# Output projection by token tile, with its norm per tile, ahead of the second FFN

## The reference

```
def modulate(h, s): return h * (1.0 + scl[:, s]) + shift[:, s]
h = swiglu(modulate(x, 0), w_ffn1_in, w_ffn1_out)
x = layer_norm(ALPHA * x + 0.5 * gate[:, 0] * h, ln_gain[0], ln_bias[0])
u = modulate(x, 1)
... # u @ w_in, pooling mixer and three attention branches
mix = concatenate([pool_out, nsa_out], axis=-1) @ w_out
x = layer_norm(ALPHA * x + gate[:, 1] * mix, ln_gain[1], ln_bias[1])
h = swiglu(modulate(x, 2), w_ffn2_in, w_ffn2_out)
x = layer_norm(ALPHA * x + 0.5 * gate[:, 2] * h, ln_gain[2], ln_bias[2])
```

## Time and profile before

| | |
|---|---|
| median of 3 runs | 1358.32 us (1356.65 to 1359.41) |
| the profiled execution, its time | 1361.54 us |
| its span in the profile | 1359.9 us |
| PE busy | 1287.4 us, 95% |
| DVE busy | 569.4 us, 42% |
| ACT busy | 445.3 us, 33% |
| POOL busy | 186.8 us, 14% |
| output projection starts | 848.3 us |
| third chunk of ffn2_in starts | 931.7 us |
| second half of FFN 2 starts | 1198.5 us |

### The profile page before, as it was taken

How to read it: one execution, slowest core, us unless ns; L and a number is a source line. 1 busy time by engine, 2 the same in 40 slices (tenths; PEclk the granted TensorE clock), 3 DMA queues, 4 the chain that set the end, 5 groups by cost and what they waited for, 6 DMA issues and landing times.

```text
span 1359.9 us, 25442 instructions
## 1 busy us (share of the span) xinstructions
PE 1287.4 (95%) x9688; PEld 1159.0 (85%) x9688; DVE 569.4 (42%) x966; ACT 445.3 (33%) x702; POOL 186.8 (14%) x369
## 2 busy tenths in 40 slices
PE   4999999999999997998879998989999999999997
PEld 3899999999999997997546666979999999988875
DVE  2422223222332366214558776584323323332466
ACT  2222222222211124224536655144222222233353
POOL 3000000000000022652372052033000000030000
PEclk8899999999999998999999999989999999999999
DMA  9544544545444343783651045222222232263463
GB/s 295 164 143 128 174 130 146 163 123 159 146 132 146 103 103 78 173 174 99 200 124 34 1 141 141 78 63 63 78 86 83 77 91 79 77 209 124 148 198 127
DMA packets 238769, 170.03 MB, mean 125 GB/s; under 512 B 46979, under 2 KB 227471, under 8 KB 238632
## 3 DMA queue, kind: packets, MB, share of 16 engines
q1 hardware_dynamic: 232159, 151.36, 38.8%
q0 software_dynamic: 6544, 17.82, 4.5%
HBM read 164.75 MB, written 8.63 MB: 128 GB/s over the span
## 4 chain that ended last, share of the span: by engine, by line
PE 86%; DVE 6%; ACT 4%; issue 1%; DVEq 1%; DMA 1%; SPq 0%; POOL 0%; POOLq 0%; ACTq 0%
PE ps L296 60%; PE ps L881 10%; PE ps L1116 3%; PE ps L2309 2%; PE ps L1125 1%; PE ps L1502 1%; PE ps L273 1%; ACT AR L1723 1%; DVE AR L2342 1%; PE ps L1610 1%; PE ps L1519 1%; DVE XT L461 1%; DVE UL L342 1%; DMA AR<-in_x_sample_dram 1%; PE ps L1573 1%
## 5 line engine op out<-in xcount | busy, mean ns | idle before, releaser
L296 PE MATMUL ps<-UH,WH 128*128 128x288 f32 x1680 | 361.0, 296 | 2.3 <-DVE WL L256 1.5
L296 PE MATMUL ps<-UH,WL 128*128 128x288 f32 x1680 | 357.9, 294 | 0.0
L296 PE MATMUL ps<-UL,WH 128*128 128x288 f32 x1680 | 357.5, 294 | 0.0
L256 DVE TENSOR_TENSOR WL<-RAW,WH 128x1024 fp32r<-128x1024 f32 x136 | 167.7, 1234 | 347.0 <-ACT WH L252 344.1
L296 PEld LDWEIGHTS ps<-UH,WH 128*128 128x128 f32 x1680 | 268.5, 188 | 2.8 <-DVE WL L256 1.8
L296 PEld LDWEIGHTS ps<-UL,WH 128*128 128x128 f32 x1680 | 269.5, 187 | 0.0
L296 PEld LDWEIGHTS ps<-UH,WL 128*128 128x128 f32 x1680 | 268.6, 188 | 0.0
L252 ACT ACTIVATE WH<-RAW 128x1024 fp32r<-128x1024 f32 x136 | 142.9, 1051 | 117.4 <-PE ps L296 109.0
L881 PE MATMUL ps<-WH,H 128*128 128x512 f32 x380 | 97.3, 398 | 0.0
L647 DVE TENSOR_TENSOR T<-MU,ps 128x576 f32<-128x576 f32 x44 | 33.2, 754 | 149.7 <-PE ps L296 149.0
L487 POOL TENSOR_TENSOR AR<-AR 128x576 f32<-128x576 f32 x12 | 19.8, 1649 | 544.9 <-ACT AR L406 482.3
(11 more groups left out here) (353 smaller groups left out, 1512.2 us busy)
## 6 DMA issues: line engine op xcount, KB each, us to landing
RAW<-in_w_ffn_in_dram SPq DMA_DIRECT2D x88, 512.0 KB, 4.9
AW<-in_w_ada_dram SPq DMA_DIRECT2D x56, 512.0 KB, 4.1
RAW<-in_w_ffn_out_dram SPq DMA_DIRECT2D x36, 512.0 KB, 3.4
AR<-in_w_ada_dram SPq DMA_DIRECT2D x7, 1024.0 KB, 10.9
RAW<-in_w_ffn_out_dram SPq DMA_DIRECT2D x16, 448.0 KB, 3.8
RAW<-in_w_in_dram SPq DMA_DIRECT2D x28, 256.0 KB, 4.1
AW<-in_w_ffn_out_dram SPq DMA_DIRECT2D x14, 512.0 KB, 3.5
AR<-in_cache_k_cmp_dram POOLq DMA_DIRECT2D x64, 64.0 KB, 2.6
```

What stands on the lines that cost most here:

```text
L256: nc.vector.tensor_tensor(WL[:, slot, :], RAW[:, slot, :], WH[:, slot, :].bitcast(F32), ALU.subtract).then_inc(split_done, 1)
L296: mm = nc.tensor.matmul(ps[:, 2 * uslot + h, 0:HT], W[:, wslot, k * P:(k + 1) * P], R[:, k0 + k, h * HT:(h + 1) * HT], start=(first and k ...
```

## The change

The output projection is done as the second half of FFN 2 is: activations stationary, weight rows moving. For each of 8 rows of weights, units 0 and 1 and the sample unit (US) get their matmuls; then unit 2 runs over all 8, then unit 3. The weights' parts lie in the place of H2 (`mix_w`), so nothing waits for a slot of WH and WL. The `turn_x` pieces move from the second half of FFN 2 to here, 3 behind each of rows 4, 5 and 6. The norm goes by unit, with the functions of the final norm: units 0, 1, then the samples, 2, 3. A new `xhat` writes the normed rows, PE turns them back to features (`early_turn`, `sample_turn`, `tile_turn`), ACT modulates them and writes UH (`rows_mod`, two instructions per feature tile, 256 columns for units 0 and 1 together, then 128 for unit 2, then 128 for unit 3), DVE writes UL (`rows_lo`). The first two chunks of ffn2_in run over 384 prompt tokens and the 64 samples, and then over the last 128 tokens (`first_rows`). The stage ln1 is gone. Gain and bias of ln1, which XT got on POOL, are applied to XA by POOL in the second half of FFN 2. The gate rows are made behind `first_pair` of w_in, for both gates (16 transposes, 4 ACT copies, 4 POOL DMAs), and 17 POOL DMAs read them back as tables before the norm. In `attn_pe`, `nat_pe` uses banks 4 to 7 and stands ahead of the wait for the pages' read-out, and two of the small transposes stand ahead of the wait for its own read-out.

```diff
-          ("w_in", 15, 8, 7), ("w_out", 8, 4, 4), ("ln1", 0, 1, 0), ("ffn2_in", 2 * FT, FT, FT),
+          ("w_in", 15, 8, 7), ("w_out", 8, 0, 0), ("ffn2_in", 2 * FT, FT, FT),
...
-        OBANK = {0: (4, 5), 1: (6, 7), 4: (4, 4), 2: (2, 3), 3: (0, 1)}
-        XA = AR2[:, 0:KT * T]
...
+                for m in range(KT):
...
+        def gate_rows_pool(pool):
+            for q, (src, _bank) in enumerate(GSRC):
+                pool.wait_ge(gt_rows, q + 1)
+                pool.dma_start(GROWS[q // 2, :, 512 * (q % 2):512 * (q % 2) + 512], src).then_inc(gt_out, 16)
...
+        def tokens_pool(pool):
+            pool.wait_ge(chunk_mm, CH0["ffn2_out"] + 2)
+            pool.wait_ge(mix_in, 16 * GATE_LOADS)
+            gain_tables(pool, 1, BX, mix_in)
+            gain_tables(pool, 2, BC, bc_in)
+            gate_tables(pool, 2, BC["gate"], BC["gate_s"], bc_in)
+            pool.wait_ge(mix_in, 16 * (GATE_LOADS + GAIN_LOADS))
+            for t in UNITS:
+                x = unit(XA, t)
+                nc.gpsimd.tensor_tensor(x, x, BX["gain" if t < 4 else "gain_s"], ALU.mult)
+                pool.drain()
+                nc.gpsimd.tensor_tensor(x, x, BX["bias" if t < 4 else "bias_s"], ALU.add).then_inc(xu_ready, 1)
...
+        def xhat(act, st, u, count):
...
+            act.wait_ge(nmr_ready, count)
+            nc.scalar.activation(unit(XA, t), unit(st.z, t), ACT.Identity, bias=NMR[:, t:t + 1],
+                                 scale=RST[:, t:t + 1]).then_inc(xh_ready, 1)
...
+        def mix_pe(pe):
...
+                src = US[:, k, :] if t == 4 else (UH, UL, UH)[q][:, k, t * P:(t + 1) * P]
+                for h in range(2):
+                    mm = nc.tensor.matmul(ps[:, OBANK[t][h] if t < 4 else 6 + h, :], src, mix_w(k, q // 2)[:, h * 512:(h + 1) * 512],
+                                          start=(k == 0 and q == 0), stop=(k == KT - 1 and q == 2))
+                return mm
...
+            for k in range(KT):
+                pe.wait_ge(hi_done, n0 + k + 1)
+                pe.wait_ge(u_split, 2 * KT + k + 1)
+                for t in (0, 1):
+                    part(k, t, 0)
+                    part(k, t, 1)
+                    if t == 0:
+                        pe.wait_ge(split_done, n0 + k + 3)
+                    mm = part(k, t, 2)
+                    if k == KT - 1:
+                        mm.then_inc(row_mm, 1)
+                        if t == 0:
+                            sample(k - 1).then_inc(chunk_mm, 1)
+                            sample(k).then_inc(row_mm, 1)
+                    elif t == 1:
+                        mm.then_inc(chunk_mm, 1)
+                if 0 < k < KT - 1:
+                    sample(k - 1)
+                if k == 4:
+                    pe.wait_ge(ln_out, KT)
+                if 4 <= k < KT - 1:
+                    for f in range(3 * (k - 4), 3 * (k - 3)):
+                        turn_x(pe, f)
+            for t in LATE:
+                if t == 2:
+                    pe.wait_ge(xa_ready, 9)
+                else:
+                    pe.wait_ge(hs_read, 1)
+                for k in range(KT):
+                    for q in range(3):
+                        mm = part(k, t, q)
+                    if k == KT - 1:
+                        mm.then_inc(row_mm, 1)
+                    j = (0 if t == 2 else KT) + k
+                    if j == 2:
+                        pair_product(pe, MIX)
+                    elif j == 6:
+                        pair_sums(pe, MIX, 0, SUMT[:, 4:5], row_sum)
+                    elif j == 8:
+                        pair_sums(pe, MIX, 1, SQT[:, 4:5], row_sq)
+                    elif j in (7, 9, 10, 11):
+                        early_turn(pe, (7, 9, 10, 11).index(j))
+                    elif j == 12:
+                        sample_turn(pe)
+                    elif j == 13:
+                        tile_turn(pe, 2, um_t, 4)
...
+        def early_turn(pe, f):
...
+                for t in range(2):
+                    mm = nc.tensor.transpose(ps[:, 2 + f % 2, (k % 2) * 256 + t * P:(k % 2) * 256 + (t + 1) * P],
+                                             XA[:, t * D + k * P:t * D + (k + 1) * P], IDN[:, :])
+            mm.then_inc(ue_t, 1)
...
+        def tile_turn(pe, t, done, count):
+            pe.wait_ge(xh_ready, count)
...
+            mm.then_inc(done, 1)
...
+        def rows_mod(act, i, j):
...
+                act.wait_ge(u_rows, j - 3)
+            nc.scalar.activation(ubuf(j), src, ACT.Identity, bias=ADA[:, SHIFT[i] + k, 0:1],
+                                 scale=ADA[:, SCALE[i] + k, 0:1]).then_inc(u32_act, 1)
+            act.drain()
+            nc.scalar.activation(UH[:, k, c0:c1], ubuf(j), ACT.Copy).then_inc(uh_rows, 1)
+        def rows_lo(dve, j):
+            k, (c0, c1) = j % KT, USPAN[j]
+            dve.wait_ge(uh_rows, j + 1)
+            nc.vector.tensor_tensor(UL[:, k, c0:c1], ubuf(j), UH[:, k, c0:c1].bitcast(F32), ALU.subtract).then_inc(u_rows, 1)
...
+        def mix_act(act):
+            for k in range(1, KT):
+                mix_hi(act, k)
+            for f, (t, h) in enumerate(XUNIT):
+                act.wait_ge(xa_t, f + 1)
+                nc.scalar.activation(unit(Z1, t)[:, h * 512:h * 512 + 512], ps[:, 4 + f % 2, :], ACT.Copy).then_inc(xa_ready, 1)
+            hi(act, *split_args("ffn2_in", 0))
+            act.wait_ge(row_mm, 5 * MIX.n + 2)
+            nc.scalar.activation(HSUM, ps[:, 6:8, :], ACT.Copy).then_inc(hs_read, 1)
+            squares_at(act, MIX, 0)
+            squares_at(act, MIX, 2)
+            xhat(act, MIX, 0, 1)
+            xhat(act, MIX, 2, 2)
+            squares_at(act, MIX, 1)
+            for j in range(4):
+                rows_mod(act, 2, j)
+            act.wait_ge(row_pair, 2 * MIX.n + 2)
+            deviation_at(act, MIX, 1, ps[:, 1, 1:2])
+            xhat(act, MIX, 1, 3)
+            rows_mod(act, 2, 4)
+            squares_at(act, MIX, 3)
+            for j in range(5, KT):
+                rows_mod(act, 2, j)
+            sample_rows_hi(act)
+            xhat(act, MIX, 3, 4)
+            hi(act, *split_args("ffn2_in", 1))
+            for j in range(KT, 2 * KT):
+                rows_mod(act, 2, j)
+            squares_at(act, MIX, 4)
+            xhat(act, MIX, 4, 5)
+            for j in range(2 * KT, 3 * KT):
+                rows_mod(act, 2, j)
+        def mix_dve(dve):
+            for k in range(1, KT):
+                mix_lo(dve, k)
+            pair_made(MIX)
+            dve.wait_ge(mix_in, 16 * GATE_LOADS)
+            dve.wait_ge(xa_ready, 9)
+            gated(dve, MIX, 0)
+            summed(dve, MIX, 0)
+            gated(dve, MIX, 2)
+            summed(dve, MIX, 2)
+            shift_at(dve, MIX, 0, 1)
+            dve.wait_ge(hs_mm, 1)
+            gated(dve, MIX, 1)
+            shift_at(dve, MIX, 2, 2)
+            summed(dve, MIX, 1)
+            lo(dve, *split_args("ffn2_in", 0)[:2])
+            dve.wait_ge(row_pair, 2 * MIX.n + 1)
+            mean_at(MIX, 1, ps[:, 1, 0:1])
+            for j in range(2):
+                rows_lo(dve, j)
+            gated(dve, MIX, 3)
+            for j in range(2, 4):
+                rows_lo(dve, j)
+            summed(dve, MIX, 3)
+            shift_at(dve, MIX, 1, 3)
+            for j in range(4, 7):
+                rows_lo(dve, j)
+            shift_at(dve, MIX, 3, 4)
+            sample_mod(dve, 2)
+            rows_lo(dve, 7)
+            sample_rows_lo(dve)
+            lo(dve, *split_args("ffn2_in", 1)[:2])
+            for j in range(KT, 2 * KT - 2):
+                rows_lo(dve, j)
+            for h in range(2):
+                gated(dve, MIX, 4, h)
+            summed(dve, MIX, 4)
+            for j in range(2 * KT - 2, 2 * KT):
+                rows_lo(dve, j)
+            shift_at(dve, MIX, 4, 5)
+            for j in range(2 * KT, 3 * KT):
+                rows_lo(dve, j)
...
+        def first_rows(pe):
...
+            for s in range(2):
+                w = (CH0[a] + s) % 2
+                pe.wait_ge(split_done, CH0[a] + s + 3)
+                for k in range(KT):
+                    if s == 0:
+                        pe.wait_ge(u_rows, KT + k + 1)
+                    for q, (W, R) in enumerate(((WH, UH), (WH, UL), (WL, UH))):
+                        nc.tensor.matmul(ps[:, 2 * s, 0:LATE_COL], W[:, w, k * P:(k + 1) * P], R[:, k, 0:LATE_COL],
+                                         start=(k == 0 and q == 0), stop=(k == KT - 1 and q == 2))
+                    if s == 1 and k == 1:
+                        tile_turn(pe, 3, ul_t, 5)
+                if s == 0:
+                    pe.wait_ge(us_rows, 1)
+                for k in range(KT):
+                    for q, (W, R) in enumerate(((WH, UH), (WH, UL), (WL, UH))):
+                        nc.tensor.matmul(ps[:, 2 * s + 1, P:P + TS], W[:, w, k * P:(k + 1) * P], R[:, k, TP:T],
+                                         start=(k == 0 and q == 0), stop=(k == KT - 1 and q == 2))
+            for s in range(2):
```

(91 more changed lines are left out.)

515 lines of the change are left out of this document (257 added, 258 removed).

## The result

The changed kernel takes 1376.2 us (median of 4 runs, 1371.9 to 1381.6), the kernel before 1358.9 beside it: ratio 1.0127, 95% interval 1.0102 to 1.0151. It is slower, as forecast, but by 17 us and not by 6, and outside the range of 1355.0 to 1369.5.

The account below looks back on a forecast made before the run. PE was taken as the bound (86% of the chain). Stretch +12.5 us (81.7 work, 13.0 waits, 1.2 clock), second half -5.0 and +0.4, pages -2.0, w_in +0.2: +6.1, so 1364.4 us against the median; range 1355.0 to 1369.5.

Parts of the forecast that it names:

- PE's work: From the projection's start to the third chunk of ffn2_in: matmuls and transposes of PE sum to 81.7 us.
- The main doubt: In first_rows: 64-column matmuls cost as much as 128-column ones, 0.11 us each, 10.6 us for 96.
- The clock: In the rebuilt stretch: 1.2 us added for a lowered clock, tied to the 6.9 us wait at unit 2's turn.
- more is lost: Rival: PE at half clock through most of first_rows and loads slower beside POOL's; +4, 1368.4 us, chance 0.12.
- The third turn of x: In the projection: PE waits 1.2 us for the weight-row splits; 2.2 with later turns, 4 if loads take 4.5.
- Unit 2's turn: At tile_turn of unit 2 in the norm: PE waits 6.9 us for ACT's xhat.
- DVE behind unit 3: Before unit 2's last rows: DVE gates and sums unit 3 ahead of the last two rows_lo; wait 2.7 us.
- Silu: Before the third chunk of ffn2_in: ACT's two Silu pieces make PE wait 0.7 us.
- The sum of the waits: All PE waits from the projection's start to the third chunk of ffn2_in: 13.0 us.
- second half: Second half of FFN 2: nine turns go, -5.0 us; unit 1 waits for DVE's last-chunk product, +0.4.
- behind the pages: From the pages' wait to the convolution: four of ten transpose groups and the small ones leave the path, -2.0 us.
- The gap in w_in: Behind the first pair of w_in: 16 gate-row transposes instead of 8 cost +0.2 us.

Follow-up runs that it names:

- e11: e8 with ACT making unit 2's xhat ahead of the samples' high part; 1355.3 us, ratio 0.9968 to the kernel before.
- e5: Kernel before plus three runs of 144 extra unused matmuls, of 64, 128 and 192 columns; 1417.5 us (one run).
- e2: Changed kernel with ACT reading out the first three turns of x before splitting the eighth weight row; 1367.3 us, ratio 1.0069.
- e12: Changed kernel with each projection weight row fetched by one DMA of 128 consecutive rows (output wrong, same work); 1370.2 us, ratio 1.0074.
- e8: e7 with early turns, samples' turn and first pair sum moved up in PE's list, ACT and DVE order following; 1355.7 us, ratio 0.9976.
- e4: Changed kernel with the samples' 64 columns joined to the late 128 in matmuls of 192; 1368.2 us, ratio 1.0065.
- e1: Changed kernel run again unaltered; 1378.1 us, ratio 1.0135 to the kernel before.
- e3: Changed kernel with POOL's 17 table DMAs held until the last weight row is split; 1373.0 us, ratio 1.0084.
- e7: Changed kernel with the edits of e2 and e4 together; 1360.2 us, ratio 1.0014 to the kernel before.
- e6: Kernel before with only the part behind the pages changed (nat_pe banks and place, two small transpose groups moved up); 1355.9 us, ratio 0.9979.
- e10: e8 with the one-DMA weight-row load of e9 added; 1378.2 us, ratio 1.0143 to the kernel before.
- e9: Changed kernel with each projection weight row fetched by one DMA into 128 partitions instead of two of 64; 1399.6 us, ratio 1.0295.

## Why the prediction was wrong in size

- **PE's work**: right. In e11, at full clock there, the projection, the turns and the products are within 0.7 us of their terms. The 384-column matmuls take 8.8 us in the changed kernel for 8.4. (Their 10.3 in e11 hold 1.4 of half clock behind the wait of 2.4, and 0.3 because some rows come from ACT and DVE one per 0.74 us.) The main doubt, 0.11 us for 64 and 128 columns, holds where the clock is full: 0.108 for 64 in the changed kernel, 0.112 for 128 in e5. The Trainium skill (TensorE: Matmul & The Clock Gate, Back-to-back issue gap) has about 81 ns per 128-column matmul in a stream of loads and matmuls; the runs of 64, 128 and 192 columns on 128 stationary ones here took 108 to 113 ns each. Its rule for the weight load (LDWEIGHTS), 107 ns, agrees with 0.108 to 0.112.
- **The clock: the step that failed.** "To these I add 1.2 for the clock." In the table above the changed kernel's rows exceed the work at full clock by about 8 us: 2.2 in the projection, 1.3 in the samples' turn, 0.8 in unit 2's, 4.0 in the last 48 matmuls. Sorted by place, 1.7 us stand behind the wait at the samples' turn and 2.6 behind the one at unit 2's turn (e2 and e12 remove the first together with its wait, e8 the second); the 4.0 stand behind the 64-column matmuls, where PE had been busy (e4, e5). The prediction had one fall of the clock, behind the wait at unit 2's turn, at less than half its price; there were three, and the dearest needs no wait. So the term of 1.2 should have been about 8, and this 7 is most of the 8.8 by which the stretch was missed. The rival "more is lost" had PE at half clock through most of `first_rows`, for +4 in all, and was given 0.12: the place was in part right (half clock over the last 48 matmuls, full clock over the 96 before), but it too was too small.
- **The third turn of x**: the mechanism was right, the load mis-sized. "3.4 us of load" came from the 2.7 of the earlier trace rows. Measured: 0.47 + 4.2. The wait was 6.0 (5.7 in e1) for 1.2, and all the waits for the turns of x 6.5 for 2.2. Three loads stand one behind the other on that chain, so 1.3 more for each is 3.9 more in all, which is nearly the difference; the prediction's own bound, 4 in all for loads of 4.5, was added up too low (three times 1.1 more makes 5.5). POOL is not the cause (e3), the two transfers of 64 partitions are (e12).
- **Unit 2's turn**: right, 6.4 for 6.9, with ACT's three waits at 1.6, 2.3 and 1.4 for 1.4, 2.2 and 1.5. ACT's rows of 256 columns took 0.95 to 0.97 us each for 1.05. e8 and e11 show that the wait is a matter of order: the same work without it.
- **DVE behind unit 3**: 0.5 for 2.7 in the profile, 1.8 in e1, 2.3 in e8 and 2.4 in e11. PE at half clock comes to it later, so that one loss covers another: in e1 the clock rises sooner behind unit 2's turn, PE reaches the first 384-column matmul 5.0 us after that turn's start for 6.3, and waits 1.3 longer for DVE's rows. For Silu there is no wait for the 0.7 forecast, and 0.6 once the clock is full (e4, e7, e8, e11).
- The sum of the waits, 13.7 for 13.0, is near by luck: the waits for the turns of x cost 4.3 more than forecast, and all the others together 3.6 less.
- **Elsewhere**: second half -5.1 for -4.6 (-3.9 in e1; the wait for slot 1 is 0.43, as forecast); behind the pages -2.1 for -2.0. The projection's start was another 1.6 early, since the clock did not fall in the 52 matmuls before it; this also happens in e6, and in e11 not. The gap in w_in took 0.2 more in this pair, as forecast (53.8 for 53.5 us around it), but e1 with the gate rows and e6 without them both have 53.0, so no cost is shown. The 0.7 between third chunk and second half is mostly the end of the lowered clock.

Open: why two transfers of 64 partitions land in 4.2 us here and in 2.7 in the kernel before. There a weight row is split every 6.3 us, so that one row's load is in flight at a time, and here the rows come 2 to 5 us apart, so that two are; no run tests this. Open too is why the clock falls in the 52 matmuls in some profiled executions and not in others with the same wait of 1.27 before them; in the same way a wait of 2.10 at unit 2's turn leaves the eight transposes at 1.10 us in e8 and is followed by 1.83 in e10. And the traces don't cover the 4.7 us by which the medians differ more than the two spans.

## What to carry to other kernels

Order the lists of three engines by when each item's input is there; here three changes of order and one joined group took the stretch from 21 us over the old form to 1.5, and each wait of 6 us cost another 1.3 to 2.6 in the clock behind it (1.3 at unit 2's turn in e1). Price the clock behind every wait and behind every run of narrow matmuls, not once. Join a run of 64-column matmuls to its neighbour: on 128 stationary columns 192 moving ones cost the 0.112 us of 128, and the run alone came with a lowered clock. Test the parts of a change alone: one small part of this one (e6) made 0.2% of the 0.3% that the best version has over the kernel before.

## What the hardware showed that was not expected

- The granted clock fell to 1.2 GHz while PE was busy throughout, in a run of 64-column matmuls: 144 took 27.2 us, 144 of 128 or 192 columns 16.2.
- DMAs over 128 partitions whose source was two separate blocks of 64 rows kept about 2 of 16 DMA engines busy, with two of them in flight (e9): 512 KB each, 18 to 19 us from issue to landing and one every 10 us, for 3.5 us where the rows were contiguous.
- Waits of 2.3 and 2.4 us in front of matmuls of 384 columns were followed by a granted clock of 0.50 (e8, e11).
